# Modulation products of a diffusion trunk in four column groups of the array, with the partial rows summed by the turning product

## The reference

```python
def adaln(cond, w, b):
    m = jax.nn.silu(cond) @ w + b
    return jnp.split(m[:, None, :], N_MOD, axis=-1)
...
def trunk(x, cond, states, on_grid, P):
    ...
        sh1, sc1, g1, sh2, sc2, g2 = adaln(cond, P['ada_w'][layer], P['ada_b'][layer])
        h = rms_norm(x, P['norm1_g'][layer]) * (1.0 + sc1) + sh1
        ...
        x = x + g1 * y
        h = rms_norm(x, P['norm2_g'][layer]) * (1.0 + sc2) + sh2
        x = x + g2 * conv_ffn(h, P['ffn_w_in'][layer], P['ffn_conv_w'][layer], P['ffn_conv_b'][layer],
                              P['ffn_w_out'][layer], on_grid)
```

## Time and profile before

| | |
|---|---|
| median of 3 runs (lowest, highest) | 4573.69 us (4571.16, 4576.46) |
| profiled execution: span | 4575.0 us |
| PE busy | 3925.4 us (86%) |
| DVE, ACT, POOL busy | 2177.4, 1019.5, 881.1 us |
| HBM read, written | 261.01 MB, 76.48 MB |

### The profile page before, as it was taken

The page is one execution under the profiler, slowest core; times in us unless marked ns, Lnnn a source line. Parts: engine busy times, 40 slices in busy tenths (PEclk is TensorE's granted clock), DMA queues, the critical chain, the costliest instruction groups (busy, mean ns, idle before and its releaser), DMA issues. The chain is left out here.

```text
span 4575.0 us, 85777 instructions
## 1 busy us (share of the span) xinstructions
PE 3925.4 (86%) x34537; PEld 3566.9 (78%) x34537; DVE 2177.4 (48%) x3748; ACT 1019.5 (22%) x1709; POOL 881.1 (19%) x708
## 2 busy tenths in 40 slices
PE   5999888377777788589999999899397789999998
PEld 3999533266666677389999999799275789999998
DVE  2433455443333454647464556400366556556555
ACT  3100243422222343412010001201144122001001
POOL 2222000000000431111222222122023202222221
PEclk8999899698898799799999999999698899999999
DMA  3222476412121221411111111222032111111111
GB/s 137 83 93 88 150 262 239 155 44 58 44 58 36 84 90 42 159 32 40 43 36 47 41 42 32 64 88 79 29 98 84 57 33 37 50 39 37 46 44 64
DMA packets 418842, 341.24 MB, mean 75 GB/s; under 512 B 62340, under 2 KB 398397, under 8 KB 416029
## 3 DMA queue, kind: packets, MB, share of 16 engines
q1 hardware_dynamic: 407137, 268.20, 19.4%
q0 software_dynamic: 10304, 60.98, 3.3%
q10 hardware_dynamic: 1152, 8.39, 0.5%
HBM read 261.01 MB, written 76.48 MB: 74 GB/s over the span
## 5 line engine op out<-in xcount | busy, mean ns | idle before, releaser
L91 POOL TENSOR_TENSOR ffn_w_lower<-ffn_w,ffn_w_upper 128x1024 fp32r<-128x1024 f32 x164 | 393.1, 2397 | 1361.2 <-DVE ffn_w_upper L86 1361.2
L931 DVE SCALAR_TENSOR_TENSOR rstd<-u_tile,ffn_taps,rstd 128x945 f32<-128x945 f32 (+3 forms) x440 | 490.3, 1114 | 85.5 <-ACT rstd L878 71.5
L99 PE MATMUL ffn_ps<-HU,ffn_w_upper 128*128 128x384 f32 x2112 | 482.0, 336 | 28.9 <-DVE ffn_w_lower L91 25.9
L99 PE MATMUL ffn_ps<-HL,ffn_w_upper 128*128 128x384 f32 x2112 | 481.1, 335 | 0.0
L99 PE MATMUL ffn_ps<-HU,ffn_w_lower 128*128 128x384 f32 x2112 | 480.7, 335 | 0.0
L99 PEld LDWEIGHTS ffn_ps<-HU,ffn_w_upper 128*128 128x128 f32 x2112 | 377.4, 189 | 31.6 <-issue 29.0
L99 PEld LDWEIGHTS ffn_ps<-HL,ffn_w_upper 128*128 128x128 f32 x2112 | 378.0, 189 | 0.0
L99 PEld LDWEIGHTS ffn_ps<-HU,ffn_w_lower 128*128 128x128 f32 x2112 | 377.8, 188 | 0.0
L99 PE MATMUL ffn_out_ps<-g_upper,ffn_w_upper 128*128 128x384 f32 x1056 | 355.7, 337 | 22.9 <-DVE g_lower L91 14.4
L99 PE MATMUL ffn_out_ps<-g_lower,ffn_w_upper 128*128 128x384 f32 x1056 | 354.6, 336 | 0.0
L99 PE MATMUL ffn_out_ps<-g_upper,ffn_w_lower 128*128 128x384 f32 x1056 | 354.5, 336 | 0.0
(11 more groups left out here) (460 smaller groups left out, 6352.3 us busy)
## 6 DMA issues: line engine op xcount, KB each, us to landing
ffn_w<-in_ffn_w_in_dram SPq DMA_DIRECT2D x88, 512.0 KB
ada_w<-in_ada_w_dram SPq DMA_DIRECT2D x40, 1024.0 KB, 5.3
rwkv_units<-unit_rows POOLq DMA_DIRECT2D x8, 2304.0 KB, 9.3
un<-rwkv_units SPq DMA_DIRECT2D x36, 512.0 KB, 3.5
z_even<-z_tile POOLq DMA_DIRECT2D x31, 576.0 KB, 3.1
in_w<-in_ab_w_in_dram SPq DMA_DIRECT2D x31, 512.0 KB
gun<-gdn_units SPq DMA_DIRECT2D x72, 192.0 KB, 3.6
z_odd<-z_tile POOLq DMA_DIRECT2D x24, 576.0 KB, 4.8
```

Source lines behind the costliest of these rows:

```text
L91: return eng.tensor_tensor(out.bitcast(F32R), x, up, ALU.subtract)
L99: mm = pe.matmul(o, w(a).bitcast(F32R), r.bitcast(F32R), start=(first and n == 0), stop=(last and n == 2))
L931: dve.scalar_tensor_tensor(out=o, in0=i, scalar=tp[:, t:t + 1], in1=o, op0=ALU.mult, op1=ALU.add).then_inc(s["conv"] if n < NCONV else s[" ...
```

## The change

`K["cond"]` becomes 128 x 8 x 32, with the two vectors in columns 0 and 1 and zeros in the other 30 (DVE clears it, ACT waits for that). The 8 matmuls of a product go round four strips of 32 PSUM partitions: c = 0 and 4 to partitions 0 to 31, c = 1 and 5 to 32 to 63, and so on. So each strip holds a partial sum in its first two rows and zeros in the others. ACT copies all 128 partitions. The turn then has all 128 rows as stationary operand and a 128 x 2 operand `quarters`, with ones at rows 0, 32, 64, 96 (column 0) and 1, 33, 65, 97 (column 1), so that it sums the four partial rows. POOL makes `quarters` with four copies out of the identity. The two slots now have a PSUM bank each, in which the turned columns lie behind the product's 256; `take` gathers them from both banks in one DVE copy. As turned columns and product share banks, the wait for `ada_cols` moves from turn 0 to product 0.

```diff
+                    for q in range(4):
+                        x = slice(q * 32, q * 32 + 32)
+                        link(pool.tensor_copy(K["quarters"][x, :], K["ident"][x, q * 32:q * 32 + 2]))
...
+                    act.wait_ge(s["cond_zeroed"], 1)
                     act.wait_ge(s["cond_turned"], 1)
-                    act.activation(K["cond"][:].rearrange("p k n -> p n k"),
+                    act.activation(K["cond"][:, :, 0:2].rearrange("p k n -> p n k"),
...
+                    dve.memset(K["cond"][:], 0.0).then_inc(s["cond_zeroed"], 1)
...
         for c in range(KD):
-            mm = pe.matmul(self.prod[self.part(k), 0:ADA_U], self.K["cond"][:, c, :], w(c), start=(c == 0), stop=(c == KD - 1))
+            q = c % 4 * 32
+            mm = pe.matmul(self.ps[q:q + 32, k, 0:ADA_U], self.K["cond"][:, c, :], w(c), start=(c < 4), stop=(c >= KD - 4))
...
-        act.activation(self.rows[0:2, k, :], self.prod[self.part(k), 0:ADA_U], ACT.Copy).then_inc(self.out[k], 1)
+        act.activation(self.rows[:, k, :], self.ps[:, k, 0:ADA_U], ACT.Copy).then_inc(self.out[k], 1)
...
-            c = 2 * (i * (ADA_U // P) + m)
-            mm = pe.matmul(self.cols[:, c:c + 2], self.rows[0:2, k, m * P:m * P + P], self.K["ident"][0:2, 0:2],
-                           start=True, stop=True)
+            c = ADA_U + 2 * (i // 2 * (ADA_U // P) + m)
+            mm = pe.matmul(self.ps[:, k, c:c + 2], self.rows[:, k, m * P:m * P + P], self.K["quarters"][:], start=True, stop=True)
...
+    def take(self, dve, to, units):
+
+        n = 2 * ADA_U // P
+        return dve.tensor_copy(to.rearrange("p (i k x) -> p k i x", k=2, x=n),
+                        self.ps[:, :, ADA_U:ADA_U + units // 2 * n].rearrange("p k (i x) -> p k i x", x=n))
...
                         if i < ADA_N:
+                            if i == 0:
+                                pe.wait_ge(s["ada_cols"], it)
                             n = half * it + i // 2
...
                         if i:
-                            if i == 1:
-                                pe.wait_ge(s["ada_cols"], it)
                             ada.turn(pe, (i - 1) % 2, half * it + (i - 1) // 2, i - 1)
```

More of the change, by code:

```diff
@@ L146, in setup_phase @@
                    "table", "cond_turned", "cond_silu", "x_turned0", "x_turned1", "x_out0", "x_out1",
-                   "dve_chain", "zeroed", "ada_in") as s:
+                   "dve_chain", "zeroed", "cond_zeroed", "ada_in") as s:
             x_in = [s["x_in0"], s["x_in1"], s["x_in2"]]
@@ L280, with __init__ @@
 class AdaUnits:
-    def __init__(self, K, s, prod, cols, rows):
-        self.K, self.prod, self.cols, self.rows = K, prod, cols, rows
+    def __init__(self, K, s, ps, rows):
+        self.K, self.ps, self.rows = K, ps, rows
         self.made, self.out = [s["made0"], s["made1"]], [s["rows0"], s["rows1"]]
         self.turned = [s["turned0"], s["turned1"]]
-    def part(self, k):
-        return slice(64 * k, 64 * k + 2)
     def product(self, pe, k, w, n):
@@ L337, in adaln_phase @@
     with ExitStack() as ctx:
-        rows = sbuf(ctx, nc, "ada_rows", [2, 2, ADA_U])
-        prod = psum(ctx, nc, "ada_prod", [P, 512])
-        cols = psum(ctx, nc, "ada_cols", [P, 512])
+        rows = sbuf(ctx, nc, "ada_rows", [P, 2, ADA_U])
+        aps = psum(ctx, nc, "ada_ps", [P, 2, 512])
         sums = psum(ctx, nc, "square_sums", [P, 3, 512])
@@ L343, in adaln_phase @@
         with phase(nc, *ADA_SEMS, "dve_chain", *SQ_SEMS) as s:
-            ada = AdaUnits(K, s, prod, cols, rows)
+            ada = AdaUnits(K, s, aps, rows)
             with nc.Block() as block:
@@ L372, in _ @@
                         dve.wait_ge(ada.turned[k], units // 2)
-                    link(dve.tensor_copy(flat[:, 0:2 * ADA_HEAD // P], cols[:, 0:2 * ADA_HEAD // P]))
+                    link(ada.take(dve, flat[:, 0:2 * ADA_HEAD // P], units))
                     adaln_finish(link, dve, K, (0, ADA_HEAD // P), [(0, 0)])
@@ L1127, in rwkv_prep_phase @@
         aw = sbuf(ctx, nc, "ada_w", [P, 2, KD, ADA_U])
-        arows = sbuf(ctx, nc, "ada_rows", [2, 2, ADA_U])
-        prod = psum(ctx, nc, "ada_prod", [P, 512])
-        cols = psum(ctx, nc, "ada_cols", [P, 512])
+        arows = sbuf(ctx, nc, "ada_rows", [P, 2, ADA_U])
+        aps = psum(ctx, nc, "ada_ps", [P, 2, 512])
         flat = K["mod"][:].rearrange("p l g k n -> p (l g k n)")
@@ L1140, in rwkv_prep_phase @@
                    "ada_in0", "ada_in1", "ada_cols", "dve_chain", *ADA_SEMS) as s:
-            ada = AdaUnits(K, s, prod, cols, arows)
+            ada = AdaUnits(K, s, aps, arows)
             dv, ac, pe_ = Steps(s["dve"], RW_DVE), Steps(s["act"], RW_ACT), Steps(s["pe"], RW_PE)
@@ L1355, in _ @@
                             n_cols = 2 * ADA_N * ADA_U // P
-                            dve.tensor_copy(flat[:, bass.ds(n_cols * it + 2 * ADA_HEAD // P, n_cols)],
-                                            cols[:, 0:n_cols]).then_inc(s["ada_cols"], 1)
+                            ada.take(dve, flat[:, bass.ds(n_cols * it + 2 * ADA_HEAD // P, n_cols)], ADA_N).then_inc(s["ada_cols"], 1)
                     dve.wait_ge(s["ada_cols"], ADA_ITS)
@@ L3266, in trunk_kernel @@
             "sel": keep("sel", 8, 8, P), "selpair": keep("selpair", 8, 4, P),
-            "PT": keep("PT", P, PT_COLS), "taps": keep("taps", P, AB_T, 3), "cond": keep("cond", P, KD, 2),
+            "PT": keep("PT", P, PT_COLS), "taps": keep("taps", P, AB_T, 3), "cond": keep("cond", P, KD, 32), "quarters": keep("quarters", P, 2),
             "mod": keep("mod", P, 2, 6, KD, 2), "gain": keep("gain", P, 2, 2, KD, 2),
```

## The result

The kernel before took 4574.89 us in the median of four runs (4571.16 to 4576.46), the changed one 4545.16 (4538.09 to 4556.42). The ratio is 0.9937, with a 95% interval of 0.9922 to 0.9952: faster by 29.7 us, where 63 were forecast. Run once more in a later job it was 4542.78 against 4581.18, ratio 0.9914 [0.9887, 0.9941]. Either way the time lies above the range of 4488 to 4542, though by less than 1 us in the later job. Counted as a gain, the later job's 38.4 us would lie inside the range (which asks for 31.7 or more), and the first job's 29.7 just outside.

The account below looks back on a forecast made before the run. PE's queue, not DVE arithmetic, was taken as the bound in the preparation. Terms 14 (head) + 22.6 (exponentials) + 24.1 (bonus) + 4.5 (inverse root) - 2 (lower clock) = 63.2 off 4573.7 gave 4511 us, range 4488 to 4542.

Parts of the forecast that it names:

- Product: One modulation product, 16 traced matmuls on four column groups at once: 1.05 us, or 1.9 at the lower clock.
- additions: New copies, memset, wider ACT copy and moved wait: costed at nothing, with small worst cases.
- head: Head stage: shorter products let the sums of squares begin at about 66; gain 14 us, 19 at the upper clock.
- The bonus: Preparation: DVE's wait for the bonus product on PE, 44.9 us, falls to 24.1, its queue 1.0 us late per iteration.
- the sign: Preparation: 1 us products with 60 us iterations would mean loads hold them, PE's ada_w waits well over 21 us.
- The exponentials: Preparation, second direction: DVE's wait for ACT's exponentials falls from 32.2 us by 4 x 2.4 to 22.6, counted as gain.
- The lower clock: Preparation: the second low-rank product at the lower clock ends late in about half the iterations, minus 2 us.
- the inverse root: Preparation, first direction: DVE's 5.0 us wait for the inverse root goes, taken as a gain of 4.5.
- Two at a time: Rival on products: only two column groups overlap; gain 42 us, total 4532; chance 0.14.
- no overlap: Rival on products: column groups do not overlap, products keep 3.45 us, total 4574; chance 0.05.
- the exposed weight loads: Rival on products: each column group's weight load waits for the matmul in flight; slower, total 4634; chance 0.04.
- Loads as the bound: Rival in the preparation: DMA with 15% left empty makes it 233 us; gain 50, total 4524; chance 0.07.

Follow-up runs that it names:

- one_strip: The changed kernel with all 8 matmuls of a product in one strip of 32 columns, all else kept: 4576.84 us, 1.0003 of the kernel before.
- noload: The changed kernel with only the first two ada_w loads of the preparation kept and reused by later products: 4526.49 us in one run, iterations 232.0.
- noload_fill: The changed kernel without 38 preparation loads, plus 60 unused matmuls per iteration to raise the clock: 4519.39 us in one run, iterations 222.0.
- the early product 3: The changed kernel with two strips and product 3 issued ahead of the second low-rank product: 4540.60 us, 0.9916 of the kernel before.
- noload_one: The changed kernel without 38 preparation loads and with all products in one strip: 4560.95 us in one run, iterations 236.7.
- noload_two: The changed kernel without 38 preparation loads and with products in two strips: 4542.98 us in one run, iterations 234.9.
- fill1: The changed kernel plus 30 unused matmuls per iteration, ahead of units 5, 7 and 9: 4538.26 us, 0.9907 of the kernel before.

## Why the prediction was wrong

**Product, additions, head: right.** 1.07 and 1.94 us for 1.05 and 1.9. one_strip shows the additions at nothing. The head gave 12.5 for 14; that the sums of squares began at 70.4 and not at 66 was partly made good by their faster second half and by product 7 at the upper clock.

**The mechanism was right, and three terms of the preparation were mis-sized.** The forecast of 220 us missed 248.2 by 28.

The bonus (24.1, measured 9.5) is the step that failed: a path that left out the loads. "Turn 6, product 8, turn 7, product 9, copy 9, turns 8 and 9 follow" took the weights as being there. They are loaded into two buffers, each load waits for the product two units before, and from product 3 on the buffer's chain is load, product, load, product. The prediction had this chain in its hands for copy 5, and did not carry it on to units 7 and 9. The queue that was to be 1.0 us late was 5.6, 5.2, 3.7 and 3.9 us late in the four iterations, and 2.1 without loads. noload shows 14 to 16 of the 28 us to be the loads. The chain also started late: product 3 was made 29.8 us into the first iteration, not 26.3, because the second low-rank product took 8.0 us for 4.2 at the lower clock. The prediction had named the sign (products of 1 us, iterations of 60, PE's waits for ada_w well over 21 us: they were 26.9), but had not put it into the sum.

The exponentials (22.6, measured 14.7). The floor was taken as 2.4 us, from the first exponential to DVE's next step. Counted from Gex1, ACT's table load of 1.28 us belongs to it, since ACT now waits at that place: 3.8, or 15.1 in all, and 5.5 us less gain. The other 2.4 are the first two iterations, where load 5 came late (waits of 5.3 and 4.7 us, 3.8 in the other two).

The lower clock (2 charged, 9.5 measured on the gates). The prediction gave the second low-rank product the lower clock, which cost 4.8 us and not 2, and left the first one at its old pace. In the profile of the change the first ones take 8.0 us in each iteration, where the kernel before had 8.0, 7.0, 5.9 and 6.4, and DVE waits 4.8 us more for them. "A lower mean clock" stood in the list of what would show it, but as a mark and not as a price for everything else on PE. noload_fill, against noload, shows that a higher clock is worth 10 us in these iterations. Of the 12 that noload leaves (232 for 220), the table load is 5.5, the bonus wait of 25.1 for 20.8 is 4.3, and the gates are 4.0 (47.6 - 41.6 = 6.0, with 2 charged); the inverse root gave 0.5 more than forecast. That makes 13.3, which is 1.3 more than there is, and the difference was not traced. That noload_fill comes out at 222, the forecast, is partly chance, since it has the table load too and gains at places where the forecast had the lower clock.

**The rivals.** Two at a time, no overlap and the exposed weight loads are refuted by the 1.07 us with its 16 loads inside 0.59. The rule of the Trainium skill (page "TensorE: Matmul & The Clock Gate", section "Part 3: Packing small matmuls — row/col tiling"), that a weight load overlaps a matmul in flight only in another row group, does not hold here: the trace disagrees, with 16 loads inside the 1.07 us of matmuls that use the same 128 rows. Its 2.38 times for three column groups stand beside 3.64 / 1.07 = 3.4 times for four. Loads as the bound (chance 0.07) had the right resource and the wrong reason: it priced bandwidth (a DMA share of 0.85), and 0.84 was indeed measured, but with the early product 3 the same loads fit into 58 us at 0.88. What bound was the time of each load in a chain. Its 4524 lay nearer to the measured 4545 than 4511 did, but by a term that no run bears out. No rival had the chain and the clock together.

## What to carry to other kernels

When a product is made faster, follow its buffer as well as its engine: with two buffers, a stretch of n products cannot be shorter than n/2 times (load + product), here 5.3 + 1.9 us a step, and that chain starts with the first product that stands behind other work. Where a change leaves TensorE with less to do, price everything else on it at the lower clock before counting the gain; here half of the column groups gave the same time. Ask of each load, too, which store it will meet when it moves. And count a floor from the event that will release it then, with what the engine does between (a table load), not from the first useful instruction of the old trace.

## What the runs showed of the hardware

- Column groups of 32 with all 128 rows in use run at once: the same 16 matmuls took 3.64 us in one strip, 1.92 in two and 1.07 in four, at the upper clock; 1.94 in four and 3.63 in two at the lower. Their weight loads ran beside them.
- In three runs without loads (noload_one, noload_two, noload) the granted clock of the preparation was 0.94 with one strip, 0.74 with two and 0.56 with four, with TensorE busy for 228, 197 and 197 of some 235 us. So in these runs shorter products took the clock from work that they don't touch, which the prediction had priced at 2 us.
- A load of 1 MB took 5.4 us in the median in the change, and 11.1 behind a store of 2304 KB (fill1).
- A stage of unchanged code, the RWKV scan, took 595 to 612 us over the profiles, the longest at a granted clock of 0.87, the shortest at 0.89. A gain of 10 us upstream could not be shown at the end with four or five runs.
